# Norming the first token tile by itself and loading the first weights ahead of the other tokens, in a two-layer hybrid decoder step

## What is computed

```
h = rmsnorm(x);  P = h @ w_in                      # 1024 x 3988, columns split among four head groups
x <- x + concat[ mLSTM(P_A) * silu(z_A), sparse_attention(P_B) * silu(z_B),
                 RWKV7(P_C) * silu(z_C), memory_attention(P_D) * silu(z_D) ] @ w_out
rms_norm(x, g) = x * rsqrt(mean(x*x) + 1e-6) * g
```

## Time and profile before

| | |
|---|---|
| median of three runs | 1571.06 us |
| the profiled execution, its own time | 1569.07 us |
| its span in the trace | 1567.4 us |
| TensorE busy | 1409.8 us, 90% |
| VectorE busy | 808.8 us, 52% |
| ScalarE busy | 406.6 us, 26% |
| mean granted TensorE clock | 0.914 of full speed |

### The profile page before, as it was taken

The page is one execution under the profiler, slowest core; times in us unless marked ns, Lnnn a source line. Parts: engine busy times, 40 slices in busy tenths (PEclk is TensorE's granted clock), DMA queues, the critical chain, the costliest instruction groups (busy, mean ns, idle before and its releaser), DMA issues.

```text
span 1567.4 us, 27948 instructions
## 1 busy us (share of the span) xinstructions
PE 1409.8 (90%) x9816; PEld 1003.5 (64%) x9816; DVE 808.8 (52%) x2032; ACT 406.6 (26%) x787; POOL 169.2 (11%) x312
## 2 busy tenths in 40 slices
PE   5998989988899998788999899998998999977795
PEld 3673777877874675454458467777888557645442
DVE  1345555766536755753126365476655675466510
ACT  4230102211122163532232201032112113545400
POOL 0000000000000264320000000000000004562000
PEclk9986899998789998799999879999977999988998
DMA  7231431421005165565142325124100323593501
GB/s 312 69 110 54 147 98 54 124 76 47 1 2 203 52 175 173 137 241 202 54 149 97 94 69 174 50 77 136 55 1 2 124 81 100 167 269 113 225 1 67
DMA packets 92927, 171.72 MB, mean 110 GB/s; under 512 B 14081, under 2 KB 79794, under 8 KB 86898
## 3 DMA queue, kind: packets, MB, share of 16 engines
q1 hardware_dynamic: 79778, 120.39, 23.4%
q0 software_dynamic: 13008, 49.54, 9.2%
HBM read 157.08 MB, written 21.12 MB: 114 GB/s over the span
## 4 chain that ended last, share of the span: by engine, by line
PE 72%; DVE 13%; issue 7%; ACT 4%; DMA 2%; SPq 0%; DVEq 0%; POOL 0%; ACTq 0%; POOLq 0%
PE bank L581 16%; PE bank L618 12%; PE bank L1186 8%; PE bank L2784 4%; PE bank L514 2%; PE bank L1320 2%; PE bank L814 2%; PE bank L2259 1%; PE bank L1212 1%; PE bank L1308 1%; DVE area L1672 1%; DMA stream<-in_winK 1%; PE bank L822 1%; PE bank L2173 1%; PE bank L2299 1%
## 5 line engine op out<-in xcount | busy, mean ns | idle before, releaser
L581 PE MATMUL bank<-stream,hT 128*128 128x512 f32 (+3 forms) x768 | 261.6, 497 | 0.5 <-DVE hT L451 0.5
L618 PE MATMUL bank<-hT,stream 128*128 128x272 f32 x960 | 230.8, 402 | 5.1 <-DVE area L1560 5.1
L618 PEld LDWEIGHTS bank<-hT,stream 128*128 128x128 f32 x960 | 186.3, 195 | 45.4 <-DVE area L1560 5.3
L581 PEld LDWEIGHTS bank<-stream,hT 128*128 128x128 f32 x768 | 145.9, 194 | 100.3 <-issue 86.7
L1186 PE MATMUL bank<-stream,prm 128*128 128x256 f32 x512 | 127.7, 412 | 0.4 <-DVE YT L1541 0.4
L2784 PE MATMUL bank<-stream,YT 128*128 128x512 f32 x256 | 114.3, 608 | 5.6 <-DVE YT L2692 5.6
L1186 PEld LDWEIGHTS bank<-stream,prm 128*128 128x128 f32 x512 | 105.8, 209 | 18.3 <-issue 1.4
L2784 PEld LDWEIGHTS bank<-stream,YT 128*128 128x128 f32 x256 | 49.5, 194 | 68.0 <-issue 62.0
L407 POOL DMA_DIRECT2D stream<-in_slcK x128 | 69.4, 552 | 168.9 <-PE bank L584 135.5
L407 POOL DMA_DIRECT2D stream<-in_slcV x128 | 68.7, 541 | 98.5 <-PE bank L2173 50.2
L2741 DVE CUSTOM_DVE_ANT_0 bank<-bank,cst 128x256 f32<-128x256 f32 (+3 forms) x96 | 45.8, 477 | 62.0 <-PE bank L2259 45.8
(11 more groups left out here) (630 smaller groups left out, 2310.6 us busy)
## 6 DMA issues: line engine op xcount, KB each, us to landing
stream<-in_cmpL SPq DMA_DIRECT2D x256, 128.0 KB, 2.2
stream<-in_win_ SPq DMA_DIRECT2D x12, 2048.0 KB, 7.3
stream<-in_slcK SPq DMA_DIRECT2D x128, 64.0 KB, 2.3
stream<-in_slcK POOLq DMA_DIRECT2D x128, 64.0 KB, 2.5
stream<-in_slcV SPq DMA_DIRECT2D x128, 64.0 KB, 4.1
stream<-in_slcV POOLq DMA_DIRECT2D x128, 64.0 KB, 4.7
stream<-in_wout SPq DMA_DIRECT2D x4, 2048.0 KB, 8.9
out_winpast<-in_winraw POOLq DMA_DIRECT2D x2, 4064.0 KB, 26.0
```

The source lines that it names most:

```text
L581: last = nc.tensor.matmul(ps[:, 0:w], hT[:, k, tok(i)], ws[:, k, :], start=(k == 0), stop=(k == KT - 1))
L618: last = nc.tensor.matmul(ps[:, 0:HALF], ws[:, k, 128 * f:128 * f + 128], hT[:, k, HALF * s:HALF * s + HALF], start=(k == 0), stop=(k == K ...
```

## The change

Two things are changed, both for the first layer only.

`act_norm` works on tile 0 as a group by itself: Square of tile 0, Ln and Exp of its one sum, its multiply; and then the squares of tiles 1 to 4, Ln and Exp of their four sums, and their multiplies. The sums of the first layer lie in column i instead of (i + 1) % 5, so that each group's columns stand together; for the second layer the columns and groups stay as they were.

SyncE issues T0, the first item of the stream, ahead of x tiles 1 to 4 and the page table. The rest of the stream follows behind the page table as before.

```diff
-        def sync_stream(sp):
+        def sync_stream(sp, todo):
             kept = {}
-            for it in items:
+            for it in todo:
...
+        def ncol(l, i):
+            return (i + 1) % 5 if l else i
+
         def act_norm(act, l):
...
-            for group in (first, (3,)) if l else (first,):
+            for group in (first, (3,)) if l else ((0,), (1, 2, 3, 4)):
                 for i in group:
...
-                    act(nc.scalar.activation(E["junk"], X[:, i, :], ACT.Square, accum_out=E["ss"][:, (i + 1) % 5:(i + 1) % 5 + 1]).then_inc(act_done, 1))
+                    act(nc.scalar.activation(E["junk"], X[:, i, :], ACT.Square, accum_out=E["ss"][:, ncol(l, i):ncol(l, i) + 1]).then_inc(act_done, 1))
                 act.wait_ge(const_in, at("const"))
-                c = slice(0, 5) if l == 0 else slice(0, 4) if len(group) > 1 else slice(4, 5)
+                c = slice(ncol(l, group[0]), ncol(l, group[0]) + len(group))
                 act(nc.scalar.activation(E["rs"][:, c], E["ss"][:, c], ACT.Ln, bias=eps, scale=1.0 / D).then_inc(act_done, 1))
                 act(nc.scalar.activation(E["rs"][:, c], E["rs"][:, c], ACT.Exp, scale=-0.5).then_inc(act_done, 1))
                 for i in (i for i in norm_order(l) if i in group):
-                    act(nc.scalar.mul(E["xn"][i], X[:, i, :], E["rs"][:, (i + 1) % 5:(i + 1) % 5 + 1]).then_inc(act_done, 1), "xn", l, i)
+                    act(nc.scalar.mul(E["xn"][i], X[:, i, :], E["rs"][:, ncol(l, i):ncol(l, i) + 1]).then_inc(act_done, 1), "xn", l, i)
...
+            sync_stream(sp, items[:1])
             for i in range(1, TILES):
                 sp.dma(f"xt{i}", sp.eng.dma_start(X[:, i, :], io["x"][:, i, :]).then_inc(x_in[i], 16), "xt", i)
             sp.dma("ptab", sp.eng.dma_start(ptab[:, :], io["ptab"]).then_inc(ptab_in, 16), "ptab")
-            sync_stream(sp)
+            sync_stream(sp, items[1:])
```

## The result

The changed kernel took 1588.71 us in the median of 20 executions (1568.90 to 1598.55), the kernel before 1570.97 in 20 beside them (1566.55 to 1580.83). The ratio is 1.0069, 95% interval 1.0048 to 1.0091. (It leaves out executions more than 1.5% above a kernel's fastest, five of the changed kernel's 20, which is why it is smaller than the ratio of the medians.) By the ratio the change costs 10.8 us. The means over all 20 are 1585.9 and 1571.7: +14.2 us. Forecast was +4.0. The profiled execution of the changed kernel took 1581.23 (span 1579.5), 12.1 us of span more than before.

The account below looks back on a forecast made before the run. TensorE, busy for 90% of the span, was taken as the bound, with its first wait at the head movable: 4.92 - 1.82 + 0.91 = +4.0 us on 1571.06 gives 1575.1 us, range 1571.0 to 1578.6.

Parts of the forecast that it names:

- Order and time of the loads: Head DMAs: full queue swaps two 2 MB blocks; T0 lands at 12.72 us, last x tile at 17.70, 4.92 later.
- ScalarE, cover of the extra group, xn1 behind x4: Head: 3.1 us of additional instructions hidden before x1, 1.9 of cover left; xn1 follows x4, taken at 23.44.
- the sum by the dearer group: Head, ScalarE: with the skill page's table-switch price the private group takes 2.8 us more, adding 0.8 us; not adopted.
- TensorE stands behind xn1: Head: tile 0's transposes run early, then TensorE waits for xn1 until 23.44; first projection 25.26 against 22.16, +3.10 us.
- The clock in the head: Head: TensorE idles, restarts at the low clock, and the first projection loses 1.24 us; net +0.91 us.
- What else moves. Nothing here: 0: Behind the head: later loads and work only shift along, layer 1 computes the same columns in the same order; 0 us.
- a lag at 60 us unlike the lag at the end: Whole run: a differing lag would show that a later wait or the clock took or added the rest.
- More clock lost: Rival: low clock through the first projection, or later low stretches on more work; +6.2 us, 1577.3; chance 0.16.
- the x tiles beside T0: Rival, head DMAs: x tiles served beside T0, x4 still near 12.8; -0.9 or -3.1 us; chance 0.08.
- the split that does what it says: Rival, head: tile 0 is projected before xn1; about -5 us, 1566; chance 0.02.
- Swallowed later: Rival: a later wait on a transfer timed from the start takes the delay back; +0 to +2 us, 1572; chance 0.13.
- The clock that stays up: Rival, head: TensorE's clock stays high through the idle stretch; +1.8 us, 1572.9; chance 0.09.
- Slower: Whole kernel: verdict that the change measures slower than no change, by 0.26%; chance 0.59.

Follow-up runs that it names:

- e11: Changed kernel with 54 unused transposes between tile 0's transposes and the wait for xn1; mean +6.6 us against the kernel before, ratio 1.0043.
- e2: Kernel before with only the order of loads changed (T0 ahead of x tiles 1 to 4), one norm group; mean +1.9 us, ratio 1.0011.
- e5: Kernel before with eight unused transposes of the identity ahead of the wait for T0; mean -1.7 us, ratio 0.9992.
- e6: Changed kernel, but TensorE waits for xn1 ahead of tile 0's transposes in the first layer; mean +6.6 us against the kernel before, ratio 1.0014.
- e17: Changed kernel with 11 useless transposes behind the first layer's T0 projections; mean +2.6 us against the kernel before, ratio 1.0016.
- e15: Kernel before with 11 useless transposes behind the first layer's T0 projections; mean +10.6 us, ratio 1.0050.
- e16: e12 without its 24 filler transposes; mean -0.9 us against the kernel before, ratio 0.9999.
- e3: Kernel before with only the norm split (tile 0 by itself), loads in the old order; mean +15.3 us, ratio 1.0098.
- e12: Changed kernel with three norm groups, tile 0 projected right behind its transposes, 24 filler transposes before T0; median 1563.22 us, ratio 0.9955 against the kernel before.
- e4: Changed kernel with tile 0 projected right behind its transposes, ahead of the wait for xn1; mean +0.6 us against the kernel before, ratio 1.0007.
- e7: The changed kernel unaltered, one more execution for a second trace; 1588.33 us.

## Why the prediction was wrong

- *Order and time of the loads*: right to 0.15 us; the queue serves 2 MB in the 5 us that the rows gave.
- *ScalarE, cover of the extra group, xn1 behind x4*: right (1.95 us of cover for 1.9; xn1 taken at 23.32 for 23.44). In the sum by the dearer group a slip: 2.8 less 1.9 us of cover is 0.9, where it says 0.8; nothing rests on it.
- *TensorE stands behind xn1*: right; the wait of 8.68 us is the one that took the place of the old. Projection at 25.29 for 25.26.
- *The clock in the head*: right (+0.91 forecast; lag 3.85 and 4.30 in two traces against the forecast 4.0). TensorE: Matmul & The Clock Gate (Part 1) in the Trainium skill says that the point at which the clock rises varies from run to run; the traces agree with 7.92 and 8.37 us for the same projection.
- *"What else moves. Nothing here: 0"*: this is the step that failed. It stands in the sum as 0 and measures some 10 us (mean +14.2, of which the head has 3.9), or 7 by the ratio (10.8 less 3.9). I had granted that layer 2 and all work behind the head issue the same instructions, and took from it that they take the same time. They do at a given clock (4.30 us of lag throughout from 240 to 320 us). But TensorE's clock in the thin stretches is not given: layer 1 took 185.0 us before, 188.5 and 196.2 in the two traces of the changed kernel, with a granted clock of 0.88, 0.86 and 0.82. That the changed head moved where the falls of the clock hit the work is the account that fits best; how it did is argued only. The prediction's own sign for such a loss, a lag at 60 us unlike the lag at the end, is what both traces show (3.85 and 12.1, 4.3 and 19.3).
- *The rival "More clock lost"* named the mechanism ("the shift puts later low stretches on more work") but priced it by the first projection alone, +3.06, and gave it 0.16. The trace of before could not show what another placement costs; it did show 185 us of work in layer 1 at a granted 0.88, of which each 0.01 more lost is some 1.9 us of full clock.
- *The other rivals*: the x tiles beside T0, and the split that does what it says, did not happen. Swallowed later: the reverse. The clock that stays up: not in this kernel; where e11 forced it, its lag of 2.06 bore out the price.
- *Slower* was right, the size was not: the median lies above the range.

Shown: the head's +3.9; that the rest is lost in clock and not in waits, in both traces of the changed kernel; that a lag as large (e2), an early burst (e5) and the split norm (e6, e17) can each be there without it; and that 1.6 us of useless work takes it away with all parts of the change in place (e17), and brings loss on in the kernel before (e15). Argued: that this goes by the place of the falls. For it, all five traces with F from 105.8 to 106.5 lose some 15 us in layer 1, and none below does; against it, F came where it was expected in only three of the last six traces, and two traces with equal F differ by 20 us. Argued too: that the eight transposes done ahead are what moves the changed kernel's F; e6, which puts them back, has ten of twelve executions under 1582 where the changed kernel has nine of 20, though its trace still loses 7.5 us beyond its lag, and e16 was to show the same narrowing and did not. The spread of F in a kernel was never measured, since there is one trace of each but two. Open: why e3 is the dearest, and what in the layers makes one placement of a fall end in 33 us of half clock and the next in none.

## What to carry to other kernels

Norming the first tile ahead is worth nothing while the engine's written order has the second tile's transposes ahead of the first projection; reorder the consumer together with the producer, and don't let the first consumer's group include the transfer that you have just pushed back. Here both together, with filler ahead, were faster by 0.45% (e12); the reorder alone (e4) and both without filler (e16) were not. Where a kernel has long thin stretches in which the granted clock goes up and down, a head change of 4 us can cost 10 to 15 us elsewhere: look at the spread of many executions and at the lag over the whole run before you credit or blame the edit. A few useless instructions, added to move the rest by one or two microseconds, help to tell such a loss from a real one; try more than one dose, since single ones missed here (e15).

## What was not expected of the hardware

TensorE had half the clock while its records show it busy for 98% of 33 us (e7, 366.5 to 399.5, 284 matmuls): a busy share near one is no sign of a full clock. Equal executions of one program differ by 30 us (1568.9 to 1598.6, of the changed kernel) on one core, with a mean granted clock of 0.917 in the fastest and 0.894 in the slowest. And 1.6 us of useless work made the changed kernel 11.6 us faster against its kernel before (mean +14.2 to +2.6; by the ratios, 8).
